# Query rows between the turns, gate columns beside the keys, and expert rows in column halves, in one step of a two-layer hybrid backbone

## The chip, the core and the metric

The kernel runs on one core of a Trainium2 chip, in one launch. Its time is the device time of one execution in microseconds. Engines are named as the profile names them: TensorE (PE, with its weight loads as PEld), VectorE (DVE), ScalarE (ACT), GpSimd (POOL) and SyncE (SP), which issues most transfers.

## What is computed

640 tokens of width 1024 (128 context tokens, 512 latent ones, five tiles of 128) go through two layers. Of each layer the parts that matter here are the input projection and the experts:

```python
h = adaln(x, norm_attn, shift, scale)          # rms norm, then modulation
p = einsum('bld,de->ble', h, w_in)             # 512 query, 128 key, 128 value, 1536 conv, 512 z,
qa, ka, va, qkvd, z, a, bt = split(p)          # 8 + 8 gate columns (a: decay, bt: beta)
g    = -exp(a_log) * softplus(a + dt_bias)
beta = sigmoid(bt)
...                                            # windowed attention, DeltaNet, output projection
# 16 experts, two for each token
hid = silu(xs @ w_gate) * (xs @ w_up)          # 1024 -> 512
y   = hid @ w_down                             # 512 -> 1024
```

Everything is float32. In the experts each operand is split into a high part (float32r) and a rest, and a product is made of three: high x high, high x low, low x high.

## The kernel before

**Projection** (`projection_phase`, helper class `Adaln`). For each of the five token tiles VectorE scales and shifts h (L364, L367), TensorE turns it in eight 128x128 pieces into PSUM banks 0 to 3 (`pe_tile`, L386), and ScalarE and VectorE copy one half each into hT (L353, L375). Then TensorE runs the column groups of w_in: query rows (`rows(QG)`, 512 columns) and key/value rows (`rows(KVG)`, 256 columns) for all five tiles (L489, banks 4 to 7), copied out by ScalarE (`take_row`, L570); twelve convolution tiles (L510, L512); the turns of queries and keys (L523, L526); the gate rows (`rows(ABG)`, 16 columns, L489); and the z rows with the sums of the squared convolution output between them (L539). SP loads the seven groups into a ring of two slots (L461), each once its slot is free: the gate group after eight convolution tiles, the z group after all twelve. Small weights follow the key group in SP's queue (L463 to L468). ScalarE's work on the gates (exp and ln, L626 to L632) follows the gate rows, and g is needed after the z rows (L546).

**Experts** (`expert_phase`). A loop over 16 experts; each expert's tokens are worked off in chunks of 128, its last chunk through a branch of its own, in which the next expert's weights are also split. There are 37 chunks in the two layers, of which five are not the last of their expert. A chunk on TensorE: 24 gate products, 24 up products (three for each of eight 128-row pieces, `product`, L1668 to L1670), four turns of the next chunk's input (L1661), four turns of hid (L1693), four more of the input, and 24 down products. ScalarE makes sg = silu(gate) (L1746), splits pieces 0 to 2 of the next expert's weights (L1721), copies hid_hi (L1751) and x_hi (L1718), splits pieces 3 and 4, copies half of y (L1757), splits piece 5 and sends y (L1762). VectorE makes the low part of piece 0 (L1777), hid = sg * up (L1795), hid_lo (L1797), x_lo (L1773), the low parts of pieces 1 and 2, its half of y (L1803) and the low parts of pieces 3 to 5. SP reloads a raw piece as soon as its low part is made (L1633). The Silu table is loaded on ScalarE ahead of sg; the other functions there are copies.

Of the kernel before, what the change touches and what calls it, by code (L numbers as in the profile page):

```python
# [20 lines left out]
P = 128  # L21
D = 1024
# [369 lines left out]
def projection_phase(nc, l, A, G, M):  # L392
# [5 lines left out]
    with ExitStack() as ctx:  # L398
# [25 lines left out]
        QG, KVG, C0G, ABG, ZG = 0, 1, 2, 5, 6  # L424
        groups = [(Q0, 512), (ATT_Q, 256)] + [(CONV0 + 512 * n, 512) for n in range(3)] + [(AB0, 16), (Z0, 512)]
# [24 lines left out]
        with nc.Block() as block:  # L450
            @block.sync
            def _(sp):
                src = A.w_in[l:l + 1].rearrange("a (k p) n -> p (a k) n", p=P)
                ada.load(sp)
                for g, (c0, n) in enumerate(groups):
                    if g >= RS:
                        if g - RS < C0G:
                            sp.wait_ge(s_["rowp"], NT * (g - RS + 1))
                        elif g - RS < ABG:
                            sp.wait_ge(s_["chan"], 4 * (g - RS - C0G + 1))  # L460
                    sp.dma_start(ring[:, g % RS, :, 0:n], src[:, :, c0:c0 + n]).then_inc(loaded[g % RS], 16)  # L461
# [17 lines left out]
            def _(pe):  # L479
                def rows(g, tiles):  # L480
                    r0 = {QG: 0, KVG: NT, ABG: 2 * NT, ZG: 3 * NT}[g]
                    for t in tiles:
                        r = r0 + t
                        if t == 0:
                            pe.wait_ge(loaded[g % RS], 16 * (g // RS + 1))
                        if r >= 4:
                            pe.wait_ge(s_["row_taken"], r - 3)
                        for k in range(KD):
                            mm = pe.matmul(G.ps[:, 4 + r % 4, 0:groups[g][1]], hT[:, k, t * P:(t + 1) * P],  # L489
                                           ring[:, g % RS, k, 0:groups[g][1]], start=(k == 0), stop=(k == KD - 1))  # L490
# [11 lines left out]
                for ct in range(CT):  # L502
                    g = C0G + ct // 4
                    if ct % 4 == 0:
                        pe.wait_ge(loaded[g % RS], 16 * (g // RS + 1))
# [24 lines left out]
                rows(ABG, range(NT))  # L530
# [13 lines left out]
                pe.wait_ge(s_["row_taken"], 4 * NT)  # L544
# [16 lines left out]
            def _(act):  # L561
                def take_row(r):
                    g, t = r // NT, r % NT
                    act.wait_ge(s_["rowp"], r + 1)
                    dst = [G.qkv[:, t, 0:ATT_Q], G.qkv[:, t, ATT_Q:], G.ab[:, t, :], G.z[:, t, :]][g]
# [54 lines left out]
                for r in range(2 * NT, 3 * NT):  # L620
                    take_row(r)
# [11 lines left out]
                for t in range(NT):  # L633
                    take_row(3 * NT + t)
# [13 lines left out]
            def _(dve):  # L648
# [71 lines left out]
                dve.wait_ge(s_["row_taken"], 3 * NT)  # L720
# [859 lines left out]
def expert_phase(nc, l, A, G, R):  # L1580
# [11 lines left out]
    with ExitStack() as ctx:  # L1592
# [10 lines left out]
        cur = ph.sb("cur_idx", [P, 1], I32)  # L1603
        raw_in = [ph.sem(f"raw_in{j}") for j in range(PIECES)]
# [5 lines left out]
        turned = G.ps[:, 2:4, :].rearrange("p b n -> p (b n)")  # L1610

# [15 lines left out]
        with nc.Block() as block:  # L1627
# [27 lines left out]
            def _(pe):  # L1655
                def turn(k, half):

                    if half == 0:
                        pe.wait_ge(gathered, k * 16 + 16)
                    for n in range(half * KD // 2, (half + 1) * KD // 2):  # L1660
                        tr = pe.transpose(turned[:, n * P:(n + 1) * P], xg[:, n:D:KD], G.c("ident"))  # L1661
                    if half:
                        tr.then_inc(xt_p, 1)

# [9 lines left out]
                turn(0, 0)  # L1674
                turn(0, 1)

                def chunk(e, k, last, final):
                    pe.wait_ge(x_lo_done, k + 1)
                    pe.wait_ge(hid_done, k + 1)
# [289 lines left out]
```

## Time and profile before

| | us |
|---|---|
| median of three runs | 2274.45 (2273.14 to 2280.45) |
| the profiled execution | 2276.08 |
| its span | 2274.4 |
| TensorE busy | 1884.7 (83%) |
| VectorE, ScalarE busy | 1246.0, 961.4 |

The span runs from the first instruction to the last. TensorE is the busiest engine, and the page's slices show where it is not: at the setup, around the start of each layer, and at each expert phase's ends.

### The profile page before, as it was taken

Reading aid. Unit: us, or ns where it says so; the run is one execution under the profiler, and the core shown is the slowest. Engines: PE = TensorE matmul, PEld = TensorE weight load, DVE = VectorE, ACT = ScalarE, POOL = GpSimd, SP = SyncE. Lnnn points to the kernel's source line nnn. Section 1 sums busy time; section 2 is a strip of 40 time slices with the busy share of each in tenths; the row PEclk is TensorE's granted clock in tenths of the full one; section 3 lists DMA queues with packets and bytes.
Section 4 is the critical chain, followed back from the end, with each engine's and each line's share of the span. In section 5 each row is a group of like instructions: output and inputs, shape, how many; then the busy total and the mean of one; then the engine's idle time right before and its main releaser. Section 6 shows DMA issues by size and latency. Waiting matters only on the chain. (4 is left out here: it accounts for less than half of the span.)

```text
span 2274.4 us, 36745 instructions
## 1 busy us (share of the span) xinstructions
PE 1884.7 (83%) x13781; PEld 1372.6 (60%) x13782; DVE 1246.0 (55%) x1769; ACT 961.4 (42%) x1375; POOL 213.3 (9%) x267
## 2 busy tenths in 40 slices
PE   5599997999698299999945999899996949999991
PEld 0255647888544177777742656488884537777771
DVE  0318315666443488686654183266663458888653
ACT  0221172334323177575522212733333337777541
POOL 0000002222100000000020000032120010000001
PEclk8599898999799599999986997999997969999996
DMA  9521107000366599797733211000004049999744
GB/s 395 214 74 38 41 1 243 11 2 3 82 247 247 205 374 377 261 370 289 277 120 119 74 39 40 0 22 2 3 3 132 28 186 374 367 370 370 289 166 167
DMA packets 96323, 376.43 MB, mean 166 GB/s; under 512 B 14479, under 2 KB 35031, under 8 KB 65479
## 3 DMA queue, kind: packets, MB, share of 16 engines
q1 hardware_dynamic: 80486, 316.76, 38.1%
q0 software_dynamic: 8496, 30.94, 3.7%
q10 hardware_dynamic: 7216, 26.97, 2.9%
q8 instruction: 91, 1.49, 0.3%
q14 instruction: 34, 0.27, 0.0%
HBM read 332.86 MB, written 41.78 MB: 165 GB/s over the span
## 5 line engine op out<-in xcount | busy, mean ns | idle before, releaser
L1777 DVE TENSOR_TENSOR expert_w_lo<-shared,expert_w_hi 128x2048 fp32r<-128x2048 f32 x192 | 430.3, 2284 | 61.7 <-ACT expert_w_hi L1721 61.7
L1721 ACT ACTIVATE expert_w_hi<-shared 128x2048 fp32r<-128x2048 f32 x192 | 359.9, 1911 | 93.8 <-PEq L141 56.5
L1668 PE MATMUL ps<-expert_w_hi,expert_x_hi 128*128 128x512 f32 x592 | 233.0, 394 | 4.9 <-DVE expert_x_lo L1773 4.9
L1670 PE MATMUL ps<-expert_w_hi,expert_x_lo 128*128 128x512 f32 x592 | 232.5, 393 | 0.0
L1669 PE MATMUL ps<-expert_w_lo,expert_x_hi 128*128 128x512 f32 x592 | 232.4, 393 | 0.0
L489 PE MATMUL ps<-shared,projection_hT 128*128 128x512 f32 (+2 forms) x640 | 218.1, 501 | 2.4 <-issue 1.7
L489 PEld LDWEIGHTS ps<-shared,projection_hT 128*128 128x128 f32 x640 | 128.6, 232 | 89.7 <-issue 84.1
L510 PE MATMUL ps<-projection_hT,shared 128*128 128x512 f32 x384 | 169.0, 593 | 0.0
L1668 PE MATMUL ps<-expert_w_hi,expert_hid_hi 128*128 128x512 f32 x296 | 120.0, 405 | 41.4 <-DVE expert_hid_lo L1797 41.4
L1668 PEld LDWEIGHTS ps<-expert_w_hi,expert_x_hi 128*128 128x128 f32 x592 | 112.5, 190 | 29.2 <-issue 5.7
L1669 PEld LDWEIGHTS ps<-expert_w_lo,expert_x_hi 128*128 128x128 f32 x592 | 112.6, 190 | 23.5
L1670 PEld LDWEIGHTS ps<-expert_w_hi,expert_x_lo 128*128 128x128 f32 x592 | 112.4, 190 | 23.6
L510 PEld LDWEIGHTS ps<-projection_hT,shared 128*128 128x128 f32 x384 | 71.1, 190 | 80.5 <-issue 80.4
L1670 PE MATMUL ps<-expert_w_hi,expert_hid_lo 128*128 128x512 f32 x296 | 116.5, 393 | 0.0
L1669 PE MATMUL ps<-expert_w_lo,expert_hid_hi 128*128 128x512 f32 x296 | 116.0, 392 | 0.0
L836 POOL TENSOR_TENSOR mixer_NTb<-mixer_Bt,consts_sb 128x256 f32<-128x256 f32 x120 | 89.1, 766 | 231.0 <-DVE mixer_Bt L1106 184.2
L1281 PE MATMUL ps<-shared,attT 128*128 128x512 f32 x160 | 77.8, 634 | 28.8 <-DMA shared<-in_w_out 28.8
L1668 PEld LDWEIGHTS ps<-expert_w_hi,expert_hid_hi 128*128 128x128 f32 x296 | 55.9, 189 | 58.8 <-issue 44.5
L660 DVE SCALAR_TENSOR_TENSOR shared<-shared,projection_cwT 128x644 f32<-128x644 f32 x96 | 85.4, 890 | 3.4
L1124 DVE TENSOR_TENSOR mixer_X<-mixer_X,ps 128x256 f32<-128x256 f32 x100 | 42.1, 421 | 76.6 <-PE ps L924 74.6
L386 PE MATMUL ps<-consts_sb,z 128*128 128x128 f32 x80 | 19.7, 427 | 76.7 <-DVE z L367 76.7
L611 ACT ACTIVATE shared<-ps 128x512 f32<-128x512 f32 x24 | 14.4, 598 | 162.4 <-PE ps L512 162.4
(329 smaller groups left out, 3175.7 us busy)
## 6 DMA issues: line engine op xcount, KB each, us to landing
shared<-in_w_gate SPq DMA_DIRECT2D x64, 1024.0 KB, 7.4
shared<-in_w_up SPq DMA_DIRECT2D x64, 1024.0 KB, 8.8
shared<-in_w_down SPq DMA_DIRECT2D x64, 1024.0 KB, 9.1
setup_m_ada_ring<-in_w_ada SPq DMA_DIRECT2D x24, 1024.0 KB, 10.5
shared<-in_w_in SPq DMA_DIRECT2D x10, 2048.0 KB, 8.4
y_table<-expert_y ACTq DMA_DIRECT2D x37, 512.0 KB, 9.1
y_table<-zero SPq DMA_DIRECT2D x1, 12800.0 KB, 41.0
qkv<-in_w_ada SPq DMA_DIRECT2D x11, 1024.0 KB, 5.0
```

Of the source, the lines that this page charges most:

```text
L386: tr = pe.transpose(self.G.ps[:, 2 * (t % 2) + half, k * P:(k + 1) * P], self.rows[:, t % self.nrow, at:at + P], self.G.c("ident"))
L489: mm = pe.matmul(G.ps[:, 4 + r % 4, 0:groups[g][1]], hT[:, k, t * P:(t + 1) * P], ring[:, g % RS, k, 0:groups[g][1]], start=(k == 0), stop ...
L510: pe.matmul(G.ps[:, 2 * (ct % 2), :], w(k), hT[:, k, P:T], start=(k == 0), stop=(k == KD - 1))
L660: ins = dve.scalar_tensor_tensor(out=out, in0=src, scalar=w, in1=out, op0=ALU.mult, op1=ALU.add)
L836: return pool.tensor_tensor(NTb[:, slot, d], Bt[:, d], row(G.c(f"level{level}_{d}"), DH), ALU.mult)
L1124: dve.tensor_tensor(X[:, d], X[:, d], blocks(d, 1), ALU.subtract).then_inc(s_["x_done"], 1)
L1281: mm = pe.matmul(G.ps[:, BO + r % NOB, :], src[:, t * P:(t + 1) * P], wo[:, k, h * 512:(h + 1) * 512], start=(k == 0), stop=(k == KD - 1))
L1668: pe.matmul(bank, hi, w_hi[:, j, w], start=first, stop=False)
L1669: pe.matmul(bank, hi, w_lo[:, j, w], start=False, stop=False)
L1670: return pe.matmul(bank, lo, w_hi[:, j, w], start=False, stop=last)
L1721: act.activation(w_hi[:, j, :], raw[:, j, :], ACT.Copy).then_inc(w_hi_done, 1)
L1777: dve.tensor_tensor(w_lo[:, j, :], raw[:, j, :], w_hi[:, j, :].bitcast(F32), ALU.subtract).then_inc(w_lo_done, 1)
```

## The change

Four things are changed, in both layers. The query rows of tile t run as soon as tile t+1 is turned. The gate columns lose their own group: they are loaded behind the key and value columns in the same ring slot and computed in the same products (272 columns), and ScalarE copies them out in that row; the z group takes the next slot. In the experts hid, its turns, hid_hi and hid_lo are made in two column halves (columns whose index modulo four is 0 or 1, then 2 or 3), the turns of the halves stand between the turns of the next input, the second half goes to PSUM bank 7, and the down products of a piece run high x high and high x low for both output halves before low x high. A one-column Silu activation stands at the head of each chunk on ScalarE.

```diff
-        QG, KVG, C0G, ABG, ZG = 0, 1, 2, 5, 6
-        groups = [(Q0, 512), (ATT_Q, 256)] + [(CONV0 + 512 * n, 512) for n in range(3)] + [(AB0, 16), (Z0, 512)]
+        QG, KVG, C0G, ZG = 0, 1, 2, 5
+        NAB = 2 * NDIR * DH
+        groups = [[(Q0, 512)], [(ATT_Q, 2 * ATT_KV), (AB0, NAB)]] + [[(CONV0 + 512 * n, 512)] for n in range(3)] + [[(Z0, 512)]]
...
-                    sp.dma_start(ring[:, g % RS, :, 0:n], src[:, :, c0:c0 + n]).then_inc(loaded[g % RS], 16)
+                    at = 0
+                    for c0, n in slices:
+                        sp.dma_start(ring[:, g % RS, :, at:at + n], src[:, :, c0:c0 + n]).then_inc(loaded[g % RS], 16)
+                        at += n
...
+                ada.pe_tile(pe, 0)
                 for t in range(NT):
-                    ada.pe_tile(pe, t)
-                pe.wait_ge(ada.act_took, NT)
-                pe.wait_ge(ada.dve_took, NT)
-                rows(QG, range(NT))
+                    if t + 1 < NT:
+                        ada.pe_tile(pe, t + 1)
+                    pe.wait_ge(ada.act_took, t + 1)
+                    pe.wait_ge(ada.dve_took, t + 1)
+                    rows(QG, [t])
                 rows(KVG, range(NT))
...
-                rows(ABG, range(NT))
                 pe.wait_ge(s_["chan_taken"], 2 * CT)
...
+                    if g == 1:
+                        act.activation(G.ab[:, t, :], G.ps[:, 4 + r % 4, 2 * ATT_KV:2 * ATT_KV + NAB], ACT.Copy)
                     act.activation(dst, src, ACT.Copy).then_inc(s_["row_taken"], 1)
...
+                ada.act_take(act, 0)
                 for t in range(NT):
-                    ada.act_take(act, t)
-                for r in range(2 * NT):
+                    if t + 1 < NT:
+                        ada.act_take(act, t + 1)
+                    take_row(t)
+                for r in range(NT, 2 * NT):
                     take_row(r)
...
-                    turn(k + 1, 0)
-                    pe.wait_ge(hid_done, k + 2)
-                    for q in range(KF):
-                        tr = pe.transpose(G.ps[:, 4, q * P:(q + 1) * P], hid[:, q:FF:KF], G.c("ident"))
-                    tr.then_inc(ht_p, 1)
-                    turn(k + 1, 1)
-                    pe.wait_ge(h_lo_done, k + 1)
+                    turn(k + 1, 0, 4)
+                    hid_turn(k, 0)
+                    turn(k + 1, 4, 6)
+                    hid_turn(k, 1)
+                    turn(k + 1, 6, KD)
...
+                        if q % HQ == 0:
+                            pe.wait_ge(h_hi_done, k * 2 + (q // HQ + 1))
                         for h in range(2):
-                            mm = product(G.ps[:, 5 + h, :], h_hi[:, at], h_lo[:, at], j, q % 2 * D + h * 512, q == 0, q == KF - 1)
+                            w = slice(q % 2 * D + h * 512, q % 2 * D + (h + 1) * 512)
+                            pe.matmul(G.ps[:, 5 + h, :], h_hi[:, at], w_hi[:, j, w], start=(q == 0), stop=False)
+                            pe.matmul(G.ps[:, 5 + h, :], h_hi[:, at], w_lo[:, j, w], start=False, stop=False)
+                        if q % HQ == 0:
+                            pe.wait_ge(h_lo_done, k * 2 + (q // HQ + 1))
+                        for h in range(2):
+                            w = slice(q % 2 * D + h * 512, q % 2 * D + (h + 1) * 512)
+                            mm = pe.matmul(G.ps[:, 5 + h, :], h_lo[:, at], w_hi[:, j, w], start=False, stop=(q == KF - 1))
...
+                    act.activation(warm[:, :], G.eps[:, :], ACT.Silu)
                     act.wait_ge(g_p, k + 1)
...
-                    act.activation(h_hi[:, :], G.ps[:, 4, :], ACT.Copy).then_inc(h_hi_done, 1)
+                    for m in range(2):
+                        act.wait_ge(ht_p, k * 2 + (m + 2))
+                        act.activation(h_hi[:, m * HQ * P:(m + 1) * HQ * P], hid_turned(m), ACT.Copy).then_inc(h_hi_done, 1)
...
-                    dve.tensor_tensor(hid[:, :], sg[:, :], G.ps[:, 1, :], ALU.mult).then_inc(hid_done, 1)
-                    dve.wait_ge(h_hi_done, k + 1)
-                    dve.tensor_tensor(h_lo[:, :], G.ps[:, 4, :], h_hi[:, :].bitcast(F32), ALU.subtract).then_inc(h_lo_done, 1)
+                    for m in range(2):
+                        dve.tensor_tensor(half_of(hid[:, :], m), half_of(sg[:, :], m), half_of(G.ps[:, 1, :], m),
+                                          ALU.mult).then_inc(hid_done, 1)
+                    for m in range(2):
+                        at = slice(m * HQ * P, (m + 1) * HQ * P)
+                        dve.wait_ge(h_hi_done, k * 2 + (m + 1))
+                        dve.tensor_tensor(h_lo[:, at], hid_turned(m), h_hi[:, at].bitcast(F32), ALU.subtract).then_inc(h_lo_done, 1)
```

`half_of(a, m)` takes columns 2m and 2m+1 of every four; `hid_turned(m)` is the first 256 columns of bank 4 (m = 0) or bank 7 (m = 1).

## Rows read from the trace of the kernel before

**Rows 1.** Table by stage: stretch, length, busy us (instructions) by engine, clock, DMA share, GB/s.

```profile
102.50:157.00 54.50, 53.98 (x160) 31.07 (x160) 0.00 (x0) 4.97 (x11) 0.00 (x0) 0.96 0.13 41
157.00:261.00 104.00, 103.95 (x384) 58.00 (x385) 70.17 (x121) 22.66 (x42) 0.00 (x0) 1.00 0.12 42
269.00:287.00 18.00, 17.85 (x81) 17.57 (x82) 0.18 (x1) 2.03 (x8) 0.00 (x0) 0.50 0.00 1
...
1402.00:1420.00 18.00, 18.00 (x70) 15.49 (x71) 1.36 (x5) 4.82 (x13) 0.00 (x0) 0.50 0.00 0
...
900.00:920.00 20.00, 18.53 (x87) 15.27 (x86) 16.59 (x10) 13.11 (x10) 1.15 (x2) 1.00 0.98 372
```

**Rows 2.** Timeline of TensorE, projection: start us, us, engine line op out<-in xcount [idle before].

```profile
90.53 1.97 PE L386 MATMUL ps<-consts_sb,z 128*128 128x128 f32 x8 [0.48 <-DVE z L367]
...
99.69 1.97 PE L386 MATMUL ps<-consts_sb,z 128*128 128x128 f32 x8 [1.08 <-DVE z L367]
102.49 54.00 PE L489 MATMUL ps<-shared,projection_hT 128*128 128x512 f32 x160 [0.83 <-issue]
...
1231.51 54.38 PE L489 MATMUL ps<-shared,projection_hT 128*128 128x512 f32 x160 [0.83 <-issue]
```

**Rows 3.** Timeline of ScalarE, first layer's projection.

```profile
111.79 0.60 ACT L570 ACTIVATE qkv<-ps 128x512 f32<-128x512 f32 x1 [10.35 <-PE ps L489]
...
139.25 0.60 ACT L570 ACTIVATE qkv<-ps 128x512 f32<-128x512 f32 x1 [6.27 <-PE ps L489]
142.71 0.38 ACT L570 ACTIVATE qkv<-ps 128x256 f32<-128x256 f32 x1 [2.86 <-PE ps L489]
...
283.02 0.18 ACT L570 ACTIVATE ab<-ps 128x16 f32<-128x16 f32 x1 [3.23 <-PE ps L489]
286.44 0.18 ACT L570 ACTIVATE ab<-ps 128x16 f32<-128x16 f32 x1 [3.23 <-PE ps L489]
...
290.47 0.22 ACT L632 ACTIVATE projection_lnb<-projection_nb 128x40 f32<-128x40 f32 x1
295.82 0.60 ACT L570 ACTIVATE z<-ps 128x512 f32<-128x512 f32 x1 [5.13 <-PE ps L489]
```

**Rows 4.** Timeline of TensorE between up and down products of one expert chunk.

```profile
902.83 0.60 PE L1661 MATMUL ps<-consts_sb,expert_xg 128*128 128x128 f32 x4
903.77 0.75 PE L1693 MATMUL ps<-consts_sb,expert_hid 128*128 128x128 f32 x4 [0.34 <-DVE expert_hid L1795]
...
906.09 0.49 PE L1668 MATMUL ps<-expert_w_hi,expert_hid_hi 128*128 128x512 f32 x1 [1.12 <-DVE expert_hid_lo L1797]
```

**Rows 5.** Timelines of VectorE, then ScalarE, around the same chunk.

```profile
883.30 0.69 DVE L1795 TENSOR_TENSOR expert_hid<-expert_sg,ps 128x512 f32<-128x512 f32 x1
...
892.24 0.69 DVE L1803 COPY expert_y<-ps 128x512 f32<-128x512 f32 x1 [0.17 <-PE ps L1670]
...
903.03 0.69 DVE L1795 TENSOR_TENSOR expert_hid<-expert_sg,ps 128x512 f32<-128x512 f32 x1 [0.72 <-PE ps L1670]
...
906.18 1.22 DVE L1773 TENSOR_TENSOR expert_x_lo<-ps,expert_x_hi 128x1024 fp32r<-128x1024 f32 x1 [0.22 <-ACT expert_x_hi L1718]
...
922.76 0.69 DVE L1795 TENSOR_TENSOR expert_hid<-expert_sg,ps 128x512 f32<-128x512 f32 x1 [3.50 <-PE ps L1670]
...
895.96 1.28 ACT L1746 ACT_TABLE_LOAD   x1 [1.33 <-issue]
...
904.64 0.60 ACT L1751 ACTIVATE expert_hid_hi<-ps 128x512 fp32r<-128x512 f32 x1 [1.05 <-PE ps L1693]
```

**Rows 6.** Waits: engine, line, whom it waited for, us in total, times, longest.

```profile
DVE expert_hid L1795 <- PE ps L1670: 42.3, 28, 10.1
```

**Rows 7.** Groups by form: busy us, mean ns of one, idle before and its releaser.

```profile
L1124 DVE TENSOR_TENSOR mixer_X<-mixer_X,ps 128x256 f32<-128x256 f32 x100 | 42.1, 421 | 76.6 <-PE ps L924 74.6
```

**Rows 8.** DMA issues 70 to 110 (KB, median us to landing), then all of L461.

```profile
shared<-in_w_in SPq DMA_DIRECT2D x1, 2048.0 KB, 13.8
...
DMA to landing us min/median/max: 2.2/8.4/16.4
```

More of the change, by code:

```diff
@@ L422, in projection_phase @@
         rt = scale[:, OUTL:OUTL + 4 * QKH * PAIRS].rearrange("p (a h n) -> p a h n", a=4, h=QKH)
-        QG, KVG, C0G, ABG, ZG = 0, 1, 2, 5, 6
-        groups = [(Q0, 512), (ATT_Q, 256)] + [(CONV0 + 512 * n, 512) for n in range(3)] + [(AB0, 16), (Z0, 512)]
+        QG, KVG, C0G, ZG = 0, 1, 2, 5
+        NAB = 2 * NDIR * DH
+        groups = [[(Q0, 512)], [(ATT_Q, 2 * ATT_KV), (AB0, NAB)]] + [[(CONV0 + 512 * n, 512)] for n in range(3)] + [[(Z0, 512)]]
+        width = [sum(n for _, n in g) for g in groups]
+        landed = [16 * sum(len(groups[o]) for o in range(g % RS, g + 1, RS)) for g in range(len(groups))]
         loaded = [ph.sem(f"in_loaded{i}") for i in range(RS)]
@@ L454, in _ @@
                 ada.load(sp)
-                for g, (c0, n) in enumerate(groups):
+                for g, slices in enumerate(groups):
                     if g >= RS:
@@ L484, in rows @@
                         if t == 0:
-                            pe.wait_ge(loaded[g % RS], 16 * (g // RS + 1))
+                            pe.wait_ge(loaded[g % RS], landed[g])
                         if r >= 4:
@@ L488, in rows @@
                         for k in range(KD):
[L489 to L490 removed]
+                            mm = pe.matmul(G.ps[:, 4 + r % 4, 0:width[g]], hT[:, k, t * P:(t + 1) * P],
+                                           ring[:, g % RS, k, 0:width[g]], start=(k == 0), stop=(k == KD - 1))
                         mm.then_inc(s_["rowp"], 1)
+                ada.pe_tile(pe, 0)
                 for t in range(NT):
[L494 to L497 removed]
+                    if t + 1 < NT:
[3 more added lines that the diff above has]
+                    rows(QG, [t])
                 rows(KVG, range(NT))
@@ L504, in _ @@
                     if ct % 4 == 0:
-                        pe.wait_ge(loaded[g % RS], 16 * (g // RS + 1))
+                        pe.wait_ge(loaded[g % RS], landed[g])
                     if ct >= 2:
@@ L619, in _ @@
                 silu(CT - 1)
-                for r in range(2 * NT, 3 * NT):
-                    take_row(r)
                 act.wait_ge(s_["silu_done"], CT)
@@ L1610, in expert_phase, with half_of, hid_turned @@
         turned = G.ps[:, 2:4, :].rearrange("p b n -> p (b n)")
+        HQ = KF // 2
+        def half_of(a, m):
+            return a.rearrange("p (n q) -> p n q", q=KF)[:, :, m * HQ:(m + 1) * HQ]
+        def hid_turned(m):
+            return G.ps[:, 4 + 3 * m, 0:HQ * P]
         def for_experts(eng, chunk):
@@ L1655, in _, with turn, hid_turn @@
             def _(pe):
-                def turn(k, half):
-                    if half == 0:
+                def turn(k, first, until):
+                    if first == 0:
                         pe.wait_ge(gathered, k * 16 + 16)
-                    for n in range(half * KD // 2, (half + 1) * KD // 2):
+                    for n in range(first, until):
                         tr = pe.transpose(turned[:, n * P:(n + 1) * P], xg[:, n:D:KD], G.c("ident"))
-                    if half:
+                    if until == KD:
                         tr.then_inc(xt_p, 1)
+                def hid_turn(k, m):
+                    pe.wait_ge(hid_done, k * 2 + (m + 2))
+                    for n in range(HQ):
+                        q = m * HQ + n
+                        tr = pe.transpose(hid_turned(m)[:, n * P:(n + 1) * P], hid[:, q:FF:KF], G.c("ident"))
+                    tr.then_inc(ht_p, 1)
                 def product(bank, hi, lo, j, col, first, last):
```

26 lines of the change are left out of this document (12 added, 14 removed).

## The prediction, made before the changed kernel had run

> **What bounds the kernel now.** The views were read in this order: the page's busy slices, the chain of waits, the table by stage, then the timelines of one projection stage and of one expert chunk. The chain that ended last holds only the closing gather and add, so the answer lies in the stages. In the projection and the experts TensorE is busy for over nine tenths of nearly every stretch, so a microsecond is worth something only where it stands in TensorE's own order. Three places stand out. First, ahead of the query rows TensorE turns five tiles of h, waiting for VectorE up to 1.08 us in each 3.05 us, then works off the five query rows; the first is ready 9.1 us after its start, then one every 6.86 us (four in 111.79 to 139.25) [rows 2, 3]. Second, the gate columns: 40 products of 16 columns hold TensorE for 17.1 us a layer (a row ends every 3.41 us, five rows), at a granted clock of 0.50 (1.2 of 2.4 GHz), in both layers [rows 1, 3]. Third, in each of the 37 expert chunks 3.26 us lie between the last up product and the first down product (902.83 to 906.09): twelve transposes, a wait of 0.34 us for hid on VectorE and one of 1.12 us for hid_lo [rows 4]. The chunk's period is 19.73 us (883.30 to 903.03, 903.03 to 922.76) [rows 5].
>
> **Query rows tile by tile.** In the new order row 0 may start when tile 1 is turned and tile 0 is taken, at 92.45 [rows 2]. Its weights were issued at 77.0 and landed 13.8 us later, at 90.8 [rows 8], so they are there. Then come row 0 (9.1, its start at half clock as now), four rows of 6.86, and three tiles still to be turned. A tile took 1.97 at half clock; at full clock I take 1.1, between 8 x 0.15 = 1.2 from the expert transposes [rows 4] and half of 1.97. End: 92.45 + 9.1 + 27.4 + 3.3 = 132.3, against 139.05 now (the fifth row's take at 139.25 less 0.2). Saved: 6.7 us. The second layer has the same shape (54.38 us of rows after 1231.51) [rows 2]; I count 6.6 for each. New waits: TensorE stands for act_took and dve_took of tile t with tile t+2's turning queued behind; both takes end a whole row earlier. VectorE now stands in its take of tile 2 until row 0 is done, with tile 4's scale and shift behind it; that tile is turned only after row 2, over 13 us later. If that cover failed, the price would be one scale and shift, some 2.5 us.
>
> **Gate columns in the key group.** Removed: 17.1 us a layer. Added: 16 columns on each of 40 key products. From the query pace 6.86 / 8 / 512 = 1.68 ns a column, so 27 ns each, 1.1 us a layer; ScalarE's five copies lie beside the products, only the last adds its start, 0.1 us. What the removed time covered: ScalarE's softplus chain ends 4.0 us after the last gate row (290.47 after 286.5) and the first z row is taken at 295.82 [rows 3]; now it can start after the last convolution tile's Silu, about 270.5, and ends near 274.5. The z rows start where the gate rows did, 286.3 - 17.1 = 269.2, and row 0 takes 9.4 us (286.3 to 295.7, half clock at first, as I leave it), so it is ready at 278.6. Covered by 4 us. The z weights were issued behind the last convolution tile; now behind the eighth of twelve, some 35 us earlier [rows 1], with 8.4 us to land at the median and 16.4 at most [rows 8]; nothing waits for them. On SP's queue the small transfer stands ahead of the convolution weights, gains and context keys, whose first reader comes after 150 us; alone in its queue it landed in 2.2 us (the minimum) [rows 8]. Nothing on the path. Net 17.1 - 1.1 - 0.1 = 15.9 a layer.
>
> **Both projections: 2 x (6.6 + 15.9) = 45.0 us.** What follows is shifted, not changed: the z stage is ScalarE's, and it starts from z row 0.
>
> **Experts, TensorE's own path.** No trace shows the half-size operations in place. VectorE's half of hid: between half of 0.69 and all of it; I take 0.42, the row of a 128x256 operation on PSUM [rows 7], since size is what changes. ScalarE's half of hid_hi: 0.38, a 128x256 copy from PSUM [rows 3]. Now the gap: four turns 902.83 to 903.43; the first half of hid is done at 903.03 + 0.42, seen at 903.50; eight more transposes of 0.15 end at 904.70. ScalarE began 0.87 after the four hid transposes began; after two it begins at 904.08, ends at 904.46, and TensorE could go at 904.6. So down starts at 904.70 instead of 906.09. hid_lo of the first half is ready at 904.9 and is wanted only after four high products, 0.9 us later. The second half's new waits have twelve products and then the next chunk behind them; hid_hi is ready near 905.1, hid_lo near 905.5, and they are wanted at 904.70 + 12 x 0.23 = 907.4. With 0.02 for waits, 1.37 us a chunk, and the period would be 18.36.
>
> **Experts, the other loop.** In a chunk that also splits the next expert's weights VectorE has its own circle: hid, hid_lo, x_lo, two splits, the copy of y; then ScalarE sends y, runs through the loop's head, loads the Silu table, makes sg and the first split, then VectorE's first split, then hid. Its slack is the idle time ahead of hid. That is 42.3 us in 28 waits [rows 6]; six are the 3.50 of chunks with no split ahead [rows 5] and one is 10.1, which leaves 11.2 us over 30 chunks, 0.37 each; at 883.30 there is none [rows 5]. The change shortens this circle only between hid and the copy of y: x_lo began 3.15 after hid (903.03 to 906.18) and begins at about 3.0, and the copy no longer waits 0.17 for TensorE. Together 0.3. Where the splits run, the period is therefore 19.73 - 0.3 - 0.37, about 19.05: saved 0.68. I count 24 of the 35 periods with splits at both ends and 11 without; each layer adds one last gap. 24 x 0.68 + 11 x 1.37 + 2 x 1.37 = 34 us.
>
> The Silu load at the chunk head is priced at nothing: it already stands right behind the loop's head, before the gate product ends (895.96, idle "issue", not a wait) [rows 5]. The added one-column activation costs ScalarE 0.1 to 0.2 us, the length of its 16-column copy (0.18) [rows 3]; the load comes earlier by the wait that it passes. Ends for the experts: if half-size operations cost as much as whole ones (0.69 and 0.60), down starts 1.0 earlier, x_lo 0.5 later, and about 15 us are left; if the second circle is no limit, 37 x 1.37 = 51.
>
> **Sum.** The profiled execution took 2276.1 us (span 2274.4), 1.6 above the median of the runs, 2274.45. 2276.1 - 45.0 - 34 = 2197; on the median's scale 2196.
>
> **Rivals.** *Only TensorE limits the experts* (chance 0.15): 45 + 51, so 2180. For it: TensorE's waits stand last in most chunks [rows 6]. Against: hid has no slack at 883.30 [rows 5].
>
> *The weights' transfers limit* (0.25): with splits the period stays near 19.73, and the experts give 13 x 1.37 = 18, so 2213. For it: the DMA engines' busy share is 0.98 at 372 GB/s between 900 and 920 [rows 1]. Against: ScalarE's splits show no wait for a landing, and a share near 1 counts overlapping packets. The Trainium skill, "DMA: Bandwidth & Descriptors", section Specifications, gives about 358 GB/s from HBM for a core and 435 GB/s for the fabric. By its first figure 7.3 MB a chunk would take 20.5 us (an estimate from that page), longer than the chunk takes now; the trace, at 372 GB/s, is already beyond it.
>
> *The clock stays at half* (0.02), the case slower than before: place, the query rows with transposes between them. A row takes 13.7 at half clock, so the five and three tiles end at 92.45 + 68.6 + 5.9 = 167, 34.6 us a layer later than forecast; if the key rows stay at half too, 18 more. Twice 52.6 gives 2302. It decides from 78 us of loss, so only once the key rows fall as well. For it: the gate rows ran at 0.50 though TensorE was busy 17.85 of 18 us [rows 1]. Against: query and key rows ran at 0.96, and chunks with twelve transposes among products at 1.00 [rows 1]. The Trainium skill, "TensorE: Matmul & The Clock Gate", Part 1, says that sustained activity releases the clock. By that rule the gate rows would have been at full speed; the trace does not agree for such narrow products.
>
> *The query order brings nothing* (0.06), for instance because row 0 waits for weights: 2197 + 13 = 2210.
>
> **How the numbers follow.** The forecast has 0.50, its own range 2188 to 2206 (0.2 us a chunk either way, and the clock's rise, which moved first rows by 0.4 us). Rivals 0.15, 0.25, 0.06, 0.02; 0.02 is left for what I don't see. The range must reach to 2180 and 2213; with the bound of 15 us for the experts, 2178 to 2216. A measurement of this kernel can tell about 0.3%, 7 us, from no change: faster 0.97, same 0.01, slower 0.02.
>
> **What would show it.** Query takes of 6.9 to 8.0 us from about 101 on; no 16-column products, key products 27 ns longer; z row 0 about 22 us earlier in each layer. In the experts: down 1.9 us after the up products instead of 3.26, hid's idle time near zero in chunks with splits, periods near 18.4 without and 19.0 with them. A wait of a split for a landing would speak for the second rival. The prediction is wrong if the periods with splits don't move, or if half operations cost as much as whole ones.

## The result, and the profile after

The changed kernel takes 2165.76 us in the median of four runs (2164.64 to 2168.01), against 2275.70 for the kernel before beside it: a ratio of 0.9516, with a 95% interval from 0.9497 to 0.9534. The forecast was 2196 with a range from 2178 to 2216: the sign was right, the gain of 110 us is 31 larger than the 79 forecast, and the time lies below the range. The profiled execution of the changed kernel took 2164.64 us, its span is 2162.9.

Where the 111.5 us between the two spans lie, read off the timelines of both traces (us, layer 1 / layer 2):

| stretch | before | after | gained | forecast |
|---|---|---|---|---|
| first turn of h to first convolution product | 69.1 / 69.5 | 60.8 / 61.4 | 8.3 / 8.2 | 5.5 |
| first convolution product to z row 0 | 138.6 / 138.8 | 120.3 / 120.7 | 18.4 / 18.1 | 17.0 |
| z row 0 to the mixer | 59.5 / 59.6 | 59.0 / 59.1 | 0.5 / 0.5 | 0 |
| mixer and tail | 430.6 / 379.7 | 424.3 / 379.5 | 6.3 / 0.2 | 0 |
| experts, first turn of the input to combine | 396.5 / 378.3 | 371.6 / 352.0 | 25.0 / 26.3 | 17 |

Together the projection gave 53.9 us (45 forecast), the experts 51.3 (34 forecast), and the first layer's mixer and tail 6.3 that no step spoke of. Now the rows, in the order of [rows 1] to [rows 6].

The table by stage of the kernel after (stretch, length, busy us by engine, clock, DMA share, GB/s): the turning of the first two tiles, query row 0, the rest of the rows, z row 0, and a steady stretch of the experts.

```profile
88.50:92.70 4.20, 3.71 (x16) 3.31 (x17) 4.16 (x4) 1.19 (x2) 0.00 (x0) 0.50 1.09 342
92.70:99.90 7.20, 7.20 (x18) 3.16 (x17) 4.24 (x4) 0.01 (x1) 0.00 (x0) 0.95 0.16 36
99.90:149.00 49.10, 48.62 (x169) 29.70 (x167) 4.49 (x5) 6.73 (x18) 0.00 (x0) 1.00 0.15 49
260.00:269.50 9.50, 9.13 (x22) 4.12 (x21) 3.56 (x15) 5.25 (x11) 0.00 (x0) 0.82 0.00 1
937.50:956.00 18.50, 18.29 (x86) 15.04 (x84) 16.93 (x13) 15.02 (x14) 1.15 (x2) 1.00 1.01 399
```

Row 0 of the query rows now runs at a clock of 0.95, where it was at 0.76 in the kernel before (its 9.11 us from 102.49), and z row 0 no longer begins behind 18 us at 0.50 [rows 1]. In the experts TensorE is busy 18.29 of 18.50 us, and the transfers run at 399 GB/s, above the 372 of [rows 1]: they were not at a limit.

The timeline of TensorE in the first projection (start, us, engine, line, operation, tiles, idle before it) answers [rows 2]:

```profile
88.50 1.97 PE L386 MATMUL ps<-consts_sb,z 128*128 128x128 f32 x8 [20.90 <-DVE z L367]
90.96 1.97 PE L386 MATMUL ps<-consts_sb,z 128*128 128x128 f32 x8 [0.48 <-DVE z L367]
92.72 7.37 PE L495 MATMUL ps<-shared,projection_hT 128*128 128x512 f32 x16
99.93 1.04 PE L386 MATMUL ps<-consts_sb,z 128*128 128x128 f32 x8
100.80 7.03 PE L495 MATMUL ps<-shared,projection_hT 128*128 128x512 f32 x16
```

From the start of row 0 on there is no wait in TensorE's order; a later tile's turn takes 0.87 us of it (99.93 to 100.80). ScalarE's timeline in the same stage answers [rows 3]: the last query row, the last key row with the gate columns beside it, the end of the softplus chain and z row 0.

```profile
130.22 0.60 ACT L579 ACTIVATE qkv<-ps 128x512 f32<-128x512 f32 x1 [6.27 <-PE ps L495]
...
148.56 0.18 ACT L578 ACTIVATE ab<-ps 128x16 f32<-128x16 f32 x1 [3.21 <-PE ps L495]
148.64 0.38 ACT L579 ACTIVATE qkv<-ps 128x256 f32<-128x256 f32 x1
...
265.38 0.22 ACT L642 ACTIVATE projection_lnb<-projection_nb 128x40 f32<-128x40 f32 x1
269.58 0.60 ACT L579 ACTIVATE z<-ps 128x512 f32<-128x512 f32 x1 [3.98 <-PE ps L495]
```

The timeline of TensorE between the up and the down products of one chunk answers [rows 4]:

```profile
937.07 0.60 PE L1679 MATMUL ps<-consts_sb,expert_xg 128*128 128x128 f32 x4
937.85 0.51 PE L1687 MATMUL ps<-consts_sb,expert_hid 128*128 128x128 f32 x2 [0.18 <-DVE expert_hid L1828]
938.20 0.39 PE L1679 MATMUL ps<-consts_sb,expert_xg 128*128 128x128 f32 x2
938.42 0.40 PE L1687 MATMUL ps<-consts_sb,expert_hid 128*128 128x128 f32 x2
938.66 0.39 PE L1679 MATMUL ps<-consts_sb,expert_xg 128*128 128x128 f32 x2
938.92 0.47 PE L1729 MATMUL ps<-expert_w_hi,expert_hid_hi 128*128 128x512 f32 x1
```

The gap is 1.85 us (937.07 to 938.92) with 0.18 of waiting in it; it was 3.26. VectorE and ScalarE around the same chunk answer [rows 5] (ACTq is ScalarE's own issue of a transfer):

```profile
937.38 0.76 DVE L1828 TENSOR_TENSOR expert_hid<-expert_sg,ps 128x256 f32<-128x256 f32 x2 [0.48 <-PE ps L1695]
940.22 1.23 DVE L1805 TENSOR_TENSOR expert_x_lo<-ps,expert_x_hi 128x1024 fp32r<-128x1024 f32 x1 [0.52 <-ACT expert_x_hi L1748]
945.76 0.69 DVE L1839 COPY expert_y<-ps 128x512 f32<-128x512 f32 x1
...
955.67 0.75 DVE L1828 TENSOR_TENSOR expert_hid<-expert_sg,ps 128x256 f32<-128x256 f32 x2 [0.29 <-PE ps L1695]
...
946.66 0.34 ACTq L1794 DMA_DIRECT2D y_table<-expert_y  x1
949.26 1.28 ACT L1774 ACT_TABLE_LOAD   x1 [2.09 <-issue]
950.56 0.20 ACT L1774 ACTIVATE expert_warm<-eps 128x1 f32<-128x1 f32 x1
950.67 0.58 ACT L1777 ACTIVATE expert_sg<-ps 128x512 f32<-128x512 f32 x1
```

One chunk takes 18.29 us (937.38 to 955.67), and hid still has idle time ahead of it, which ends with TensorE's up product. Of the 35 periods 17 lie between 18.29 and 18.31 us, the longest is 18.86, and the means of the two layers are 18.45 and 18.38. The waits of VectorE for the up product, which answer [rows 6], are hardly fewer than before:

```profile
DVE expert_hid L1828 <- PE ps L1695: 34.0, 26, 10.2
```

TensorE's own waits for hid are 0.17 to 0.19 us in 31 of the 35 periods, and longer in four (0.25, and 0.71 to 0.73 three times). So the second circle, which the forecast had as the limit wherever the next weights are split, limits few of these chunks.

### The profile page after: what moved, and what is told of

It reads as the page before. It is cut to its first block and busy times, and to the rows that moved or that the text cites. A ratio compares the mean times of both kernels' runs of the same rounds, so it can differ in the third digit from the quotient of the medians.

```text
span 2162.9 us, 36690 instructions
## 1 busy us (share of the span) xinstructions
PE 1829.2 (85%) x13621; PEld 1328.0 (61%) x13622; DVE 1251.1 (58%) x1843; ACT 968.5 (45%) x1449; POOL 213.2 (10%) x267
## 5 line engine op out<-in xcount | busy, mean ns | idle before, releaser
L495 PE MATMUL ps<-shared,projection_hT 128*128 128x512 f32 (+1 forms) x480 | 181.6, 536 | 0.7 <-ACT kT L448 0.7
L495 PEld LDWEIGHTS ps<-shared,projection_hT 128*128 128x128 f32 x480 | 92.4, 194 | 82.9 <-issue 75.4
L1735 PE MATMUL ps<-expert_w_hi,expert_hid_lo 128*128 128x512 f32 x296 | 91.3, 390 | 0.0
L1679 PE MATMUL ps<-consts_sb,expert_xg 128*128 128x128 f32 x312 | 54.8, 282 | 37.0 <-DMA expert_xg<-h_table,expert_cur_idx 37.0
L1054 ACT ACTIVATE mixer_T<-ps 128x256 f32<-128x256 f32 x100 | 38.4, 384 | 100.0 <-PE ps L934 95.9
## 6 DMA issues: line engine op xcount, KB each, us to landing
setup_m_ada_ring<-in_w_ada SPq DMA_DIRECT2D x24, 1024.0 KB, 10.5
```

The source lines that it names most:

```text
L495: mm = pe.matmul(G.ps[:, 4 + r % 4, 0:width[g]], hT[:, k, t * P:(t + 1) * P], ring[:, g % RS, k, 0:width[g]], start=(k == 0), stop=(k == K ...
L1735: mm = pe.matmul(G.ps[:, 5 + h, :], h_lo[:, at], w_hi[:, j, w], start=False, stop=(q == KF - 1))
```

## The experiments

All times stand beside runs of the kernel before on the same chip (medians 2273.2 to 2275.2, and 2275.7 beside the changed kernel), so a difference of 2 us between two of the experiments says nothing. "Stage" below is the length of the experts' stage as in the table, read from the trace.

**e1, only the query order** (`pe_tile` of tile t+1, the two waits for tile t, row t; ScalarE's `act_take` and `take_row` likewise).

```diff
+                ada.pe_tile(pe, 0)
                 for t in range(NT):
-                    ada.pe_tile(pe, t)
-                pe.wait_ge(ada.act_took, NT)
...
+                    if t + 1 < NT:
+                        ada.pe_tile(pe, t + 1)
+                    pe.wait_ge(ada.act_took, t + 1)
...
+                    rows(QG, [t])
```

> The kernel before with only the query rows moved between the turns. The prediction's step: 6.6 us a layer, 13 us in all, about 2262. Read from the changed kernel's trace: convolution starts 7.9 and 8.2 us earlier in the two layers, so 16 us, about 2259, with the clock up within 1 us of row 0's start. Rival, that the earlier rise of the clock there depends on the other edits: 10 us or less, and row 0 takes about 9 us as before. Rival, the order brings nothing: 0.

Measured: 2253.83 us, ratio 0.9915 (0.9901 to 0.9928), 19 us less. The convolution starts 9.6 and 10.5 us earlier after the first turn of h; row 0's 7.24 us ran at a clock of 0.98. So the order brings half as much again as forecast, and without the other edits. The theory of 16 us had been read from the changed kernel, where the key rows are 1.1 us longer by the gate columns (five times 3.67 instead of 3.45 us); that counts against the gate edit.

**e2, only the gate columns** (groups, `take_row` and the ring's slots as in the change).

```diff
-        groups = [(Q0, 512), (ATT_Q, 256)] + ... + [(AB0, 16), (Z0, 512)]
+        groups = [[(Q0, 512)], [(ATT_Q, 2 * ATT_KV), (AB0, NAB)]] + ... + [[(Z0, 512)]]
...
-                rows(ABG, range(NT))
```

> The kernel before with only the gate columns in the key group (and the z group in the next slot). The prediction's step: 15.9 us a layer, 32 us in all, about 2243. Read from the changed kernel's trace: z row 0 no longer runs at half clock, which adds about 2.2 us a layer: 36 us, about 2239, with z row 0 taken some 18 us earlier. Rival: without the new query order the clock does not come up before the z rows, and 32 us remain.

Measured: 2238.06 us, ratio 0.9844 (0.9830 to 0.9857), 35 us less. From the first convolution product to z row 0 it takes 120.4 and 121.1 us instead of 138.6 and 138.8. The 18.0 us of each layer are the 17.1 of the gate rows and about 1 us of z row 0, whose stretch is at a higher clock (0.80 from 269.36 to 278.02 in e2, 0.75 from 286.5 to 295.7 before). The theory's 2.2 us for z row 0 are too many. The rival falls: z row 0 gains without the new query order.

**e3, both edits of the projection.** The diff is that of e1 and e2 together.

> The kernel before with both edits of the projection and none of the experts'. The prediction's step: 45 us, about 2230. Theory from the changed kernel's trace: 26.2 and 26.7 us of projection, about 53 us, and the mixer and the tail of layer 0 keep their times: 2222. Rival: the 6.3 us that layer 0 loses between mixer and experts in the changed kernel hang on where the projection ends (the clock's phase): 59 us, 2216.

Measured: 2216.92 us, ratio 0.9751 (0.9737 to 0.9764), 56 us less; the two edits add up to within 2 us (19.4 and 35.2). In the trace the projections give the 53 us of the theory, and mixer and tail of layer 1 take 426.3 us where they took 430.6: part of the rival's 6.3 us is there without any edit of the experts. In e4, with the old projection, they take 431.0.

**e4, only the experts' edits** (hid in halves, turns, order of the down products, Silu at the head of the chunk).

> The kernel before with the whole change of the experts and none of the projection's. The prediction's step: periods of 19.05 us where the next weights are split, 34 us, about 2241. Theory from the changed kernel's trace: periods of 18.3 to 18.5 us, TensorE's own path everywhere, 49 to 50 us, about 2225. If the 6.3 us of layer 0 between mixer and experts came with the experts' edit (another place of code or data), 56 us, 2219.

Measured: 2222.18 us, ratio 0.9779 (0.9765 to 0.9792), 51 us less; stages of 370.2 and 352.0. The edits of the experts do the same with and without those of the projection, and the two sums, 56 and 51, make 107 of the 110 of the whole. The prediction's 34 is out.

**e5, the changed kernel without the one-column Silu.**

```diff
-                    act.activation(warm[:, :], G.eps[:, :], ACT.Silu)
                     act.wait_ge(g_p, k + 1)
                     act.wait_ge(hid_done, k * 2 + 1)
                     act.activation(sg[:, :], G.ps[:, 0, :], ACT.Silu).then_inc(sg_done, 1)
```

> The changed kernel without the one-column Silu at the head of each chunk. Theory, as the prediction priced it: the table load stands ahead of the gate product's end in any case, so nothing changes: periods of 18.3 to 18.5 us, 2166 us. Rival: it is this Silu that shortened the way from ScalarE's sending of y to the table load (3.27 to 2.74 us); without it the periods with splits go back by 0.5 us, 24 times: 12 us more, 2178.

Measured: 2179.45 us, ratio 0.9588 (0.9575 to 0.9601): 14 us more than the changed kernel, the rival's number, though not by its mechanism. The timelines of ScalarE and VectorE, and the two lines of TensorE that follow them:

```profile
949.79 0.34 ACTq L1793 DMA_DIRECT2D y_table<-expert_y  x1
953.54 1.28 ACT L1776 ACT_TABLE_LOAD   x1 [3.02 <-PE ps L1695]
954.83 0.60 ACT L1776 ACTIVATE expert_sg<-ps 128x512 f32<-128x512 f32 x1
...
957.27 2.29 DVE L1808 TENSOR_TENSOR expert_w_lo<-shared,expert_w_hi 128x2048 fp32r<-128x2048 f32 x1 [1.09 <-ACT expert_w_hi L1751]
959.48 0.74 DVE L1827 TENSOR_TENSOR expert_hid<-expert_sg,ps 128x256 f32<-128x256 f32 x2
...
959.95 0.50 PE L1687 MATMUL ps<-consts_sb,expert_hid 128*128 128x128 f32 x2 [0.63 <-DVE expert_hid L1827]
```

The table load waits for the gate product (3.02 us of idle time that TensorE ended); in the kernels before and after it waits for nothing but the issue ([rows 5], and 949.26 above). From the gate product's end the load, sg, the first split, its low part and hid then follow one another without a gap, hid comes 0.45 us later for TensorE than in the changed kernel (a wait of 0.63 instead of 0.18), its down products begin another 0.23 later, and nearly all periods with splits at both ends are 18.98 or 18.99. In the kernel before the load stood ahead of the wait without any help. What moved it is the change's own count of hid: two for each chunk, so that the second wait's value has to be worked out anew. In the record of ScalarE's sequencer that register operation holds the wait for the gate product (953.46), and the load stands behind it (953.54). The Trainium skill, "ScalarE: Activation LUTs", section "Step-by-step: what each stage is for", says that the compiler places the load right before the activation that needs it. The trace agrees, and shows what that costs when a wait stands there: 0.68 us a chunk.

**e6, hid undivided, the order of the down products kept.**

```diff
-        HQ = KF // 2
+        HALVES, HQ = 1, KF
...
-                    turn(k + 1, 4, 6)
-                    hid_turn(k, 1)
-                    turn(k + 1, 6, KD)
+                    turn(k + 1, 4, KD)
```

> The changed kernel with hid, its turns, hid_hi and hid_lo undivided; the order of the down products (high rows first) stays. Theory: TensorE's path is the limit, and of the 1.43 us saved in a chunk the order alone keeps what lay between the end of hid_hi and the end of hid_lo, about 0.8, and the halves bring the other 0.6: periods near 18.9 us, 37 times 0.6 is 22 us more, 2188. Rival, the order does everything: 2166. Rival, the halves do everything: 51 us more, 2217.

Measured: 2183.39 us, ratio 0.9607 (0.9594 to 0.9621): 18 us more than the changed kernel, and steady periods of 18.89 to 18.91, so 0.6 each. TensorE's first down product in its timeline:

```profile
943.28 0.47 PE L1727 MATMUL ps<-expert_w_hi,expert_hid_hi 128*128 128x512 f32 x1 [0.33 <-ACT expert_hid_hi L1781]
```

**e7, the down products in their old order, hid in halves.**

```diff
+                        if q % HQ == 0:
+                            pe.wait_ge(h_lo_done, k * 2 + (q // HQ + 1))
                         for h in range(2):
-                            ...
+                            mm = product(G.ps[:, 5 + h, :], h_hi[:, at], h_lo[:, at], ...)
```

> The changed kernel with the down products in their old order (high by high, high by low, low by high for one output half after the other), so that hid_lo of each half is wanted ahead of its first product. Theory, from the prediction's own working: hid_lo of the first half is there 0.2 us after TensorE has ended its transposes, that of the second in time: 0.2 us a chunk, 8 us more, 2174. Rival, the new order is worth nothing once there are halves: 2166. Rival, both halves of hid_lo come late: 0.5 us or more a chunk, 2185 or above.

Measured: 2179.53 us, ratio 0.9587 (0.9574 to 0.9601): 14 us more than the changed kernel, and steady periods of 18.73 to 18.77. The same product:

```profile
943.28 0.47 PE L1693 MATMUL ps<-expert_w_hi,expert_hid_hi 128*128 128x512 f32 x1 [0.34 <-DVE expert_hid_lo L1826]
```

Both parts are needed: with the order alone TensorE waits 0.33 us for hid_hi, with the halves alone 0.34 for hid_lo. The theory had 0.2 a chunk for e7 and the periods show 0.46: TensorE is free to start 1.54 us after hid and not 1.67 (937.38 to 938.92 in the changed kernel), and hid_lo lets it start after 2.01 and not 1.87 (941.27 to 943.28 in e7).

**e8, a delay in the second circle of the changed kernel.**

```diff
+                    for _i in range(4):
+                        act.activation(pad[:, _i * P:(_i + 1) * P], G.c("ident"), ACT.Copy)
                     act.activation(warm[:, :], G.eps[:, :], ACT.Silu)
```

> The changed kernel with four copies of 128x128 (about 0.27 us each, 1.1 together) on ScalarE at the head of each chunk, inside the circle of VectorE and ScalarE and off TensorE's path. Theory: this circle has little slack left, 0.1 to 0.5 us by the idle time ahead of hid; the periods with splits grow by 0.6 to 1.0 us, those without not at all: some 19 us more, 2185. Rival, only TensorE's path counts and the circle has over 1 us to spare: no change, 2166.

Measured: 2236.78 us, ratio 0.9838 (0.9823 to 0.9853), 71 us more. The size of the delay was misjudged: a load was placed ahead of the copies too, and a second one behind them:

```profile
889.00 1.28 ACT L1776 ACT_TABLE_LOAD   x1 [1.40 <-issue]
...
891.21 1.28 ACT L1777 ACT_TABLE_LOAD   x1
```

So 2.2 us were added and not 1.1 (the text of e10 below has 2.4). Most periods with splits are between 20.1 and 21.8. That the circle has over 1 us to spare is out; how much it has, e10 tells.

**e9, the two waits exchanged, no Silu at the head.**

```diff
-                    act.activation(warm[:, :], G.eps[:, :], ACT.Silu)
-                    act.wait_ge(g_p, k + 1)
                     act.wait_ge(hid_done, k * 2 + 1)
+                    act.wait_ge(g_p, k + 1)
```

> The changed kernel without the one-column Silu, and with ScalarE's two waits ahead of sg exchanged: first for hid of the chunk before, then for the gate product. In e5 the table load started only after the gate product's end (9.69 to 5.94 us ahead of hid, no idle time left ahead of hid). Theory: what the Silu at the chunk head brings is the place of the load ahead of the wait for the gate product, nothing else; with the exchanged waits the load stands there again without it, periods go back from 18.98 to 18.3 to 18.5 us and the time to 2166, or 1 to 3 us below, as the Silu's own 0.1 us a chunk is gone. Rival, the Silu itself is needed (the load stays behind the wait, or sg is slow without it): 2179 as in e5.

Measured: 2164.39 us, ratio 0.9528 (0.9515 to 0.9541): the changed kernel's time, within the uncertainty. ScalarE's timeline:

```profile
947.00 0.34 ACTq L1793 DMA_DIRECT2D y_table<-expert_y  x1
949.73 1.28 ACT L1776 ACT_TABLE_LOAD   x1 [2.24 <-issue]
951.02 0.60 ACT L1776 ACTIVATE expert_sg<-ps 128x512 f32<-128x512 f32 x1
```

The load waits for the issue alone again, without the Silu. Its place was the whole worth of that Silu.

**e10 and e11, a smaller delay in the same circle, after and before.** Two Silus of 128x512, ahead of the wait for the gate product (in e10 in place of the one-column Silu).

```diff
+                    for _i in range(2):
+                        act.activation(pad[:, _i * FF:(_i + 1) * FF], G.const[:, 0:FF], ACT.Silu)
                     act.wait_ge(g_p, k + 1)
```

> The changed kernel with two Silus of 128x512 in place of the one-column Silu at the head of each chunk on ScalarE: 0.9 us more in the circle of VectorE and ScalarE (e8 had added 2.4, as a second table load came with its copies), nothing on TensorE. Theory: the circle's slack is the idle time ahead of hid, 0.1 to 0.5 us a chunk, 0.25 in the mean; periods with splits of about 18.9, 0.65 in some 28 of them, 18 us more: 2184. Rival, slack of 0.9 or more: 2166. Rival, no slack at all: 0.9 each, 25 us more, 2191.

> The kernel before with two Silus of 128x512 at the head of each chunk on ScalarE: 1.0 us more in the same circle. The prediction's step: slack of 0.37 a chunk with the way from the sending of y to the table load fixed at its length of before (3.27 us in the mean); 0.63 more in some 30 periods, 19 us: 2293. Theory from e5 to e7, where that way was 2.6 to 2.8 us as soon as the phase of the chunk moved: slack of 0.72 at its short length, periods of 20.0, 0.28 in 30 periods, 8 us more: 2282. Rival, slack of 1.0 or more: 2274.

Measured: e10 2185.66 us, ratio 0.9613 (0.9598 to 0.9627), 20 us more than the changed kernel. Its steady periods in layer 1 are 18.85 to 18.89, so 0.56 of the 0.9 came through and 0.34 was slack, near the theory's 0.25:

```profile
922.85 0.75 DVE L1830 TENSOR_TENSOR expert_hid<-expert_sg,ps 128x256 f32<-128x256 f32 x2
941.71 0.75 DVE L1830 TENSOR_TENSOR expert_hid<-expert_sg,ps 128x256 f32<-128x256 f32 x2
```

In layer 2 the steady ones are 18.95 to 19.07, which leaves a slack of 0.13 to 0.25. e11 took 2292.08 us, ratio 1.0082 (1.0066 to 1.0097), 19 us more than before, just what the prediction's step gives. But its trace does not bear that step out. TensorE's waits for hid in the kernel before and in e11:

```profile
PE ps L1693 <- DVE expert_hid L1795: 13.0, 37, 0.5
...
PE ps L1694 <- DVE expert_hid L1798: 28.1, 37, 2.2
```

They grew by 15.1 us, so of 30 times 1.04 us (the table load lies 6.98 us ahead of hid, where 5.94 is the least in the kernel before) only 15 came through, and the slack was about 0.53 a chunk. Most of the rest of the 25 us by which the experts' stages are longer in e11's trace is TensorE's clock (that execution took 2301.3 us, 9 above the median). The table by stage around one chunk:

```profile
905.00:913.60 8.60, 6.87 (x36) 5.58 (x34) 4.94 (x4) 8.34 (x9) 0.18 (x1) 1.00 1.01 426
913.62:917.03 3.41, 2.88 (x7) 2.33 (x8) 3.19 (x3) 2.39 (x2) 0.96 (x1) 0.50 0.99 410
917.03:920.45 3.42, 3.42 (x17) 2.82 (x16) 2.84 (x2) 1.92 (x1) 0.00 (x0) 1.00 0.65 186
```

TensorE's two waits in it, from its timeline:

```profile
911.83 0.75 PE L1694 MATMUL ps<-consts_sb,expert_hid 128*128 128x128 f32 x4 [1.16 <-DVE expert_hid L1798]
914.15 0.79 PE L1669 MATMUL ps<-expert_w_hi,expert_hid_hi 128*128 128x512 f32 x1 [1.12 <-DVE expert_hid_lo L1800]
```

In the middle of a stage at full speed, and right at these two waits, the granted clock is 0.50 (1.2 GHz of 2.4) for a stretch, and TensorE takes 20.70 us from this wait for hid to the next, where the chunks without such a stretch take 19.36 to 19.40. Eight such stretches lie in e11's expert stages, of which seven cost 1.3 to 1.6 us and one 2.8, each at a pair of waits, for hid (0.47 to 2.25 us) and for hid_lo (1.12). The waits do not decide it alone: in 16 other chunks of e11, with 0.46 to 1.44 us for hid and the same wait for hid_lo, no such stretch follows; in the 13 with 0.34 or 0.35 us there is none either. One lay in the stages of the kernel before, where the period was 21.33 instead of 19.73, and none in those of the changed kernel. The executions of e11 at the median left no trace; that their 19 us are the 15 of waits and two or three such stretches is an estimate from these numbers.

**e12, a later reload of one piece of weights, in the kernel before.**

```diff
-                        sp.wait_ge(w_lo_done, e * PIECES + (j + 1))
+                        sp.wait_ge(w_lo_done, e * PIECES + (j + 1 + (j == 3)))
```

> The kernel before, in which SyncE issues the reload of the fourth piece of weights (half of up) one low part later, some 2.3 us, so that it no longer falls beside ScalarE's loop head. Theory: the reads of ScalarE's loop head are slow (0.6 to 1.4 us instead of 0.3) when such an issue lies beside them; without it the way from the sending of y to the table load is 2.6 to 2.8 us instead of 3.27 in the mean. Rival: it is the reads of two engines at one time, and the mean stays over 3.1. The time hardly moves in either, since TensorE's own path limits the chunk before the change: 2270 to 2276.

Measured: 2272.21 us, ratio 0.9998 (0.9989 to 1.0008). From the sending of y to the table load it takes 3.17 us in the mean, 3.27 before: the theory falls, this issue of SyncE is not what makes ScalarE's loop head long. In the sequencer's record of e12 no read of the loop head lies beside an issue of SyncE (24 of 98 did before), and those beside a read of VectorE still take 0.61 us in the mean, the others 0.33 (0.72 and 0.33 before). The rival alone is not enough either: in the changed kernel 56 reads lie beside one of VectorE, and they take 0.38.

## Why the prediction was wrong, point by point

The spans gained 111.5 us where 79 were forecast. Of the difference 17 us lie in the experts (51.3 for 34), 9 in the projections (53.9 for 45) and 6 in the first layer's mixer and tail (6.3 for nothing).

**Query rows: the mechanism was right, two sizes were off.** 6.7 us were forecast; e1 shows 9.6 and 10.5. "9.1, its start at half clock as now" was the larger miss: row 0 took 7.2 us. TensorE was at 0.50 in both kernels while it turned tiles ([rows 2], and the first line of the table by stage), and the clock came up 0.7 and 1.7 us after row 0's start in the two layers instead of 4.3 and 5.1. The later tiles took 0.87 us each and not 1.1, which is 0.7 for three. 6.7 + 1.9 + 0.7 = 9.3. No cover failed: VectorE's late scale and shift cost nothing.

**Gate columns: right, and 1 us a layer too careful.** 17.1 was removed, the key rows grew by 1.1 as forecast, the softplus chain is done at 265.6, 4.0 us ahead of z row 0's copy (4 forecast), and the z weights are waited for nowhere. What was missed is z row 0, which no longer follows 18 us at half clock: its stretch is at 0.82, where it was at 0.75.

**The experts: the step that failed is the second circle's slack and length.** TensorE's own path came out as worked out: a gap of 1.85 us where 1.87 to 1.9 stood, periods of 18.30 where 18.36 stood. But the period of 19.05 for chunks with splits was wrong; that circle was shorter than the step put it, by three pieces.

First, the slack. It was taken as the idle time ahead of hid, 0.37 us. That idle time has a ceiling, 0.72 us where splits run: where the table load is early, sg waits for the gate product instead, and what the circle has left over appears ahead of sg, on ScalarE. This row of the kernel before, from its waits, was not read:

```profile
ACT expert_sg L1746 <- PE ps L1670: 16.1, 14, 4.8
```

Of these 16.1 us 3.5 lie in the 30 chunks that the prediction counted, 0.12 each. The whole slack can be read in that same trace: the table load never starts less than 5.94 us ahead of hid, and in these 30 chunks it starts 6.51 ahead in the mean, so 0.57 early. e11 puts the slack at about 0.53. Second, the copy of y came 0.55 us earlier after hid (8.39 instead of 8.94 us: 937.38 to 945.76, and [rows 5]), where 0.3 was counted: the halves let x_lo begin at 2.85 and TensorE ends its down products well ahead of the copy. Third, the way from the sending of y to the table load, taken as fixed, fell from 3.27 to 2.74 us in the mean. By e10 the circle is 18.30 - 0.34 = 17.96 us long, 0.34 below TensorE's path; with 19.73 - 0.53 = 19.2 before, it lost 1.24 us (1.0 to 1.15 by the second layer's periods in e10), and the second and third piece are 1.08. So the rival "only TensorE limits the experts" is what happened: 51 us by its working, 51.3 in the spans, 51 in e4.

**The Silu at the chunk head was priced at nothing, and is worth 14 us (e5).** The reason given, that the load "already stands right behind the loop's head", is a fact of the kernel before. The halves of the same change take it away by their doubled count, and the Silu (or e9's exchange of waits) gives it back. The edits were priced one by one against the kernel before; this one should have been priced in the kernel that it stands in.

**The other rivals.** The weights' transfers do not limit: 399 GB/s and periods of 18.30 with splits. The clock did not stay at half. That the query order brings nothing is refuted by e1.

**What stays open.** Of the 6.3 us of the first layer's mixer and tail 4.3 are there with both edits of the projection and none of the experts' (before 430.6, e1 428.5, e2 426.4, e3 426.3, e4 431.0 us); the second layer shows nothing of it. Matched instruction by instruction, the traces before and after part in three places: 2.0 us in the first 36 us of the mixer, 1.3 at the start of the output projection, and 3.4 at eight of its later products. The last of them, before and then after:

```profile
723.33 1.06 PE L215 MATMUL ps<-kvrows,condT 128*32 128x512 f32 x8 [2.96 <-DMA kvrows<-in_w_ada]
724.33 5.40 PE L1281 MATMUL ps<-shared,qkvT 128*128 128x512 f32 x8
...
691.95 1.07 PE L215 MATMUL ps<-kvrows,condT 128*32 128x512 f32 x8 [1.41 <-DMA kvrows<-in_w_ada]
692.95 3.70 PE L1291 MATMUL ps<-shared,qkvT 128*128 128x512 f32 x8
```

The eight products ran at a mean granted clock of 0.68 before and at 1.00 after, and the wait for a transfer ahead of them was 1.55 us longer before. Of the 2 us that e3 lacks, 1.7 are one more stretch at 0.50 (around 611 us); e7, with the projection of the changed kernel, has such a stretch too and takes 426.0. So a good part of the 6.3 us hangs on where TensorE's stretches at half clock fall, and no edit was aimed at that: it is luck. Why they fall elsewhere, and what the 2.0 us at the mixer's start are, is not shown.

Nor is the cause of the shorter way to the table load: it is 3.17 to 3.37 us in the mean in the five kernels with the old chunk (before, e1, e2, e3, e12) and in e11, and 2.70 to 2.92 in the changed kernel, e4, e6, e7, e9 and e10 (3.06 in e8; 3.84 in e5, where the load stands behind the wait). So it goes with the down products' order or the halves (either will do, e6 and e7), but e12 excludes the one cause that was tried, and its rival alone does not explain it.

## What to carry to other kernels

Slack that is read as idle time ahead of one instruction can have a ceiling: follow the same circle back over each engine in it and add the waits that its other members have for the same bound. When several edits come together, price each in the kernel that holds the others, above all one that seems to do nothing: ask which of the others would take away what hides it. And look where a table load stands among the waits of the activation that needs it.

## What the runs showed of the hardware

Short waits in a dense stretch can cost more than themselves: in e11 a wait of 0.5 to 2.3 us and one of 1.1, close together, eight times went with a stretch at a granted clock of 0.50 that cost 1.3 to 1.6 us more (2.8 in one case); in 16 other chunks with such waits the clock stayed up. The Trainium skill, "TensorE: Matmul & The Clock Gate", section "A second HAM failure mode: psum-queue depth-cycling", describes such small pauses between groups of products letting the clock go down and up; the trace agrees for eight of the 24 chunks with such waits.

On ScalarE a turn of the loop costs 2.3 to 4.1 us, in the kernels before and after, between the issue of its last transfer and the next load (2.60 in the rows of the changed kernel above), nearly all of it work on registers: in the sequencer's record each of three reads of a table takes 0.27 to 0.30 us at best and up to 1.37.
